# Feed-forward output projection by seven half-size products, with the sums of weights made in DRAM

## The reference, cut to what matters

```
def swiglu(h, w_in, w_out):
    gate, up = jnp.split(h @ w_in, 2, axis=-1)
    return (jax.nn.silu(gate) * up) @ w_out
...
    x = x + 0.5 * swiglu(rmsnorm(x, norm_ffn1[layer]), w_ffn1_in[layer], w_ffn1_out[layer])
```

## Time and profile before

| | us |
|---|---|
| median of 3 runs (1964.11 to 1965.36) | 1964.17 |
| the profiled execution's own time | 1964.59 |
| its span (first to last instruction) | 1962.6 |
| TensorE busy | 1942.2 |
| VectorE busy | 1442.0 |
| ScalarE busy | 891.0 |
| GpSimd busy | 222.1 |

### The profile page before, as it was taken

How to read it: one execution, slowest core, us unless ns; L and a number is a source line. 1 busy time by engine, 2 the same in 40 slices (tenths; PEclk the granted TensorE clock), 3 DMA queues, 4 the chain that set the end, 5 groups by cost and what they waited for, 6 DMA issues and landing times.

```text
span 1962.6 us, 23667 instructions
## 1 busy us (share of the span) xinstructions
PE 1942.2 (99%) x9192; PEld 1616.2 (82%) x9192; DVE 1442.0 (73%) x1815; ACT 891.0 (45%) x1245; POOL 222.1 (11%) x166
## 2 busy tenths in 40 slices
PE   8999999999999999999999999999999999999998
PEld 7888888888888888888888888888897898888886
DVE  7988844886767859898833889883368778988722
ACT  6555632352434435555621555562168445554510
POOL 0000012000000031000021000002146440000121
PEclk9999999999999999999999999999999999999999
DMA  5243122331313320422232242223222014222331
GB/s 173 86 144 114 60 103 91 128 134 43 135 43 134 127 88 12 155 92 86 89 104 86 99 155 92 86 89 103 85 85 86 1 61 155 86 86 101 104 101 60
DMA packets 76188, 189.52 MB, mean 97 GB/s; under 512 B 4144, under 2 KB 12336, under 8 KB 73008
## 3 DMA queue, kind: packets, MB, share of 16 engines
q1 hardware_dynamic: 76080, 188.04, 27.4%
HBM read 185.92 MB, written 2.10 MB: 96 GB/s over the span
## 4 chain that ended last, share of the span: by engine, by line
PE 89%; DVE 6%; issue 2%; ACT 1%; DMA 1%; POOL 1%; SPq 0%; DVEq 0%; ACTq 0%; POOLq 0%
PE bank L2455 12%; PE bank L2457 12%; PE bank L2456 12%; PE bank L2447 12%; PE bank L2449 12%; PE bank L2448 12%; PE bank L2677 3%; PE bank L2675 3%; PE bank L2676 3%; PE bank L2556 2%; DVE part_lo L1567 1%; PE bank L2686 1%; PE bank L2936 1%; PE bank L2875 1%; DVE quad_w L1729 1%
## 5 line engine op out<-in xcount | busy, mean ns | idle before, releaser
L1025 ACT ACTIVATE part_hi<-quad_w 128x1024 fp32r<-128x1024 f32 x280 | 293.3, 1064 | 278.5 <-PE bank L2457 194.5
L1567 DVE TENSOR_TENSOR part_lo<-quad_w,part_hi 128x1024 fp32r<-128x1024 f32 x280 | 330.4, 1221 | 23.6 <-ACT part_hi L1025 23.4
L2447 PE MATMUL bank<-gated_hi,out_hi 128*128 128x512 f32 x704 | 274.8, 390 | 0.0
L2449 PE MATMUL bank<-gated_hi,out_lo 128*128 128x512 f32 x704 | 274.0, 389 | 0.0
L2448 PE MATMUL bank<-gated_lo,out_hi 128*128 128x512 f32 x704 | 273.9, 389 | 0.0
L2455 PE MATMUL bank<-part_hi,s_hi 128*128 128x512 f32 x640 | 252.3, 394 | 1.1 <-DVE part_lo L1567 1.1
L2457 PE MATMUL bank<-part_hi,s_lo 128*128 128x512 f32 x640 | 249.4, 390 | 0.0
L2456 PE MATMUL bank<-part_lo,s_hi 128*128 128x512 f32 x640 | 249.2, 389 | 0.0
L2455 PE MATMUL bank<-part_hi,xn_hi 128*128 128x512 f32 x608 | 237.4, 390 | 2.8 <-DVE part_lo L1567 2.8
L2457 PE MATMUL bank<-part_hi,xn_lo 128*128 128x512 f32 x608 | 236.6, 389 | 0.0
L2456 PE MATMUL bank<-part_lo,xn_hi 128*128 128x512 f32 x608 | 236.6, 389 | 0.0
(11 more groups left out here) (306 smaller groups left out, 3522.9 us busy)
## 6 DMA issues: line engine op xcount, KB each, us to landing
quad_w<-w_ffn_in SPq DMA_DIRECT2D x80, 1024.0 KB, 7.4
out_raw<-w_ffn_out SPq DMA_DIRECT2D x64, 704.0 KB, 4.1
quad_w<-w_ret_in SPq DMA_DIRECT2D x14, 1024.0 KB, 7.4
rest_raw<-w_ffn_in SPq DMA_DIRECT2D x32, 256.0 KB, 5.3
quad_w<-w_ret_in SPq DMA_DIRECT2D x16, 512.0 KB, 5.3
quad_w<-w_ret_out SPq DMA_DIRECT2D x8, 1024.0 KB, 5.3
w_raw<-w_dsa SPq DMA_DIRECT2D x7, 1024.0 KB, 4.8
x_res<-x_in SPq DMA_DIRECT2D x8, 256.0 KB, 6.7
```

The source lines that it names most:

```text
L1025: nc.scalar.activation(in_four(part_hi[part_slot(h)]), source, copy).then_inc(part_hi_made, 1)
L1567: nc.vector.tensor_tensor(in_four(part_lo[part_slot(h)]), source, in_four(part_hi[part_slot(h)]).bitcast(FP32), ALU.subtract)\
L2447: mm(to, w_hi_of[:, at:at + width], hi, start=start, stop=False)
L2449: return mm(to, w_lo_of[:, at:at + width], hi, start=False, stop=stop)
```

## The change

The output product becomes a Strassen scheme too (`OUT_PRODUCTS`, seven products), with halves of the features (11 tiles), of the tokens (256) and of the output columns (4 chunks, `OUT_TILES`). A product is 4 steps (`out_step`), one for each chunk, of 11 tiles x 3 matmuls with 256 tokens moving. Of the seven left factors three are plain quarters of the activations and four are sums; VectorE makes the sums (`sum_left`) and the low parts, ScalarE the high parts. Of the seven right factors three are plain quarters of `w_out`; four are sums of quarters (`T_SUMS`), and no engine computes them. GpSimd issues, for each, one transfer that copies a quarter (or an earlier sum) from DRAM to DRAM and, when it has landed, one that adds a second quarter onto it in DRAM. They start in the input stage. The output stage then loads 28 units of 128 x 1408, from `w_ffn_out` or from `t_sums`, into ten places of memory (`OUT_PLACES`). Three chains of products gather in PSUM, two chunks of 256 tokens to a bank, and 14 or 16 instructions of VectorE (`add_out`) bring them to the residual, some with a minus sign. Squares for the next norm are made by ScalarE (`square`), and summed by VectorE (`add_square`), in three of the four feed-forwards; in the last one GpSimd still squares the first 4 chunks. At the end of the stage VectorE's order is: the last `add_out`, `stream_lo` of chunks 6 and 7, two squares, and then the next stage's first weights (before the attention stage, the unit of 128 x 2048).

```diff
+OUT_PRODUCTS = ("x11w11", "x12w21", "S1T1", "S2T2", "S3T3", "x22T4", "S4w22")
+T_SUMS = ("S1T1", "S2T2", "S3T3", "x22T4")
+T_TERMS = {"S1T1": ("w11", "w12"), "S2T2": ("S1T1", "w22"), "S3T3": ("w12", "w22"), "x22T4": ("S2T2", "w21")}
+OUT_PLACES = "AIBC" + "DEGH" + "ABCD" + "EGHA" + "BCGJ" + "EDFC" + "ABFC"
...
+    t_sums = nc.dram_tensor("t_sums", (SUBLAYERS.count("ffn") * len(T_SUMS) * OUT_TILES, P, OUT_UNIT), FP32).ap()
...
+                if s == 0:
+                    pool.wait_ge(part_lo_made, parts_through(f, 0, PRODUCTS.index("S4w22")))
+                for name in T_SUMS:
+                    first, second = T_TERMS[name]
+                    source = t_units(f, first) if first in T_SUMS else quarter_units(f, first)
+                    nc.gpsimd.dma_start(t_units(f, name), source, max_dma_last_dim=4 * OUT_UNIT)\
+                        .then_inc(t_copied, 16)
+                    pool.wait_ge(t_copied, t_count(f, name))
+                    nc.gpsimd.dma_start(t_units(f, name), quarter_units(f, second), accum_op=ALU.add,
+                                        max_dma_last_dim=4 * OUT_UNIT).then_inc(t_summed, 16)
+                    pool.wait_ge(t_summed, t_count(f, name))
...
+                    if name in T_SUMS and dt == 0:
+                        sp.wait_ge(t_summed, t_count(f, name))
+                    load_out_unit(i)
...
+                    for k in range(HALF_TILES):
+                        if dt == 0 and k in batches:
+                            pe.wait_ge(left_lo_made, left_count(f, p, batches.index(k)))
+                        left_hi_k, left_lo_k = cols(left_hi[p % 2], k, HALF_SEQ), left_low_tile(p, k)
+                        first_in, last_in = opens and k == 0, closes and k == HALF_TILES - 1
+                        w_hi_k, w_lo_k = hi[:, k * P:(k + 1) * P], lo[:, k * P:(k + 1) * P]
+                        mm(to, w_hi_k, left_hi_k, start=first_in, stop=False, skip_group_check=joins)
+                        mm(to, w_hi_k, left_lo_k, start=False, stop=False, skip_group_check=joins)
+                        done = mm(to, w_lo_k, left_hi_k, start=False, stop=last_in, skip_group_check=joins)
+                    done.then_inc(unit_done, 1)
```

More of the change, by code:

```diff
@@ new lines, in add_out @@
+                def add_out(name, p, piece, part, factor):
+                    (a, b), chain = piece, chain_of(p)
+                    n, first = out_bank(s, chain, a)
+                    columns, tokens = {"x11": (0, 0), "x12": (1, 0), "x21": (0, 1), "x22": (1, 1)}[name]
+                    x = x_res[:, :].rearrange("p (k t) -> p k t", k=CHUNKS)
+                    to = x[:, OUT_TILES * columns + a:OUT_TILES * columns + b,
+                           HALF_SEQ * tokens:HALF_SEQ * (tokens + 1)]
+                    made = bank[n][:, :].rearrange("p (d t) -> p d t", d=2)[:, first:first + b - a]
+                    dve.wait_ge(unit_done, u0 + OUT_TILES * p + b)
+                    done = nc.vector.scalar_tensor_tensor(to, made, factor, to, ALU.mult, ALU.add)
+                    if part is None:
+                        done.then_inc(x_updated, b - a)
+                    else:
+                        done.then_inc(x_added, 1)
@@ new lines, in _ @@
+                out_low(14)
+                out_low(15)
+                for piece in pieces(s, "Z")[1:]:
+                    add_out("x22", 2, piece, "P5", 0.5)
+                left_low(4, 0)
+                out_low(16)
+                left_low(4, 1)
+                out_low(17)
+                sum_left("S4")
+                add_out("x12", 3, two[0], "P6", -0.5)
+                out_low(18)
+                out_low(19)
+                add_out("x12", 3, two[1], "P6", -0.5)
+                left_low(5, 0)
@@ new lines, in _ @@
+                for i in range(OUT_STEPS):
+                    if s == len(SUBLAYERS) - 1 and i == OUT_STEPS - 1:
+                        final = ("norm", len(SUBLAYERS))
+                        pe.wait_ge(squares_done, squares_before(final) + square_ops(final))
+                        for b in range(BLOCKS):
+                            done = mm(bank[STAT_BANK][:, b:b + 1], tile(square_sum, b), ones[:, :1],
+                                      start=True, stop=True)
+                        done.then_inc(stat_done, 1)
+                    out_step(i)
+                    if i in (0, 2):
+                        turn(GROUPS - 1, i // 2)
```

602 lines of the change are left out of this document (402 added, 200 removed).

## The result

The kernel after takes 1997.08 us (median of 4 runs, 1994.67 to 2000.22) where the kernel before takes 1964.37 in runs beside it: 1.0166 times as long, 95% interval 1.0149 to 1.0184. I had forecast 1930 and a range up to 1990. It is slower, by 1.7%. The profiled execution has a span of 1992.8 us against 1962.6: 30.2 more.

What follows compares the result with a forecast made beforehand. TensorE was taken as the bound, with work in flight for 1942.2 of 1962.6 us. 1964.59 - 36.3 (matmuls) + 1.7 (seam) = 1930.0 us, with the transfers in DRAM counted as hidden; range 1923 to 1990.

Steps and rivals of the forecast that it cites:

- Matmuls, 9.1 us a stage: Output stages: 924 matmuls at 0.1197 us replace 528 at 0.2267, a gain of 9.1 us a stage, 36.3 in all.
- VectorE, 13.4 to 14.2 of 15.8 us: Output stage: VectorE's work per middle product, 13.4 to 14.2 us, fits in TensorE's 15.8 us, so no stall.
- two thin covers: Output stage: VectorE readies the second product's activations 1 to 2 us early and the fifth's bank about 1 us early.
- the rival in which VectorE binds: Output stage: three-dimensional operands or thin covers cost VectorE 5 to 10%, 3 to 8 us a stage, 1940 to 1965; chance 0.17.
- The step that doesn't halve: Rival: output matmuls take 0.1295 us or more, the change gains nothing or loses, 1964 to 1975; chance 0.04.
- The sums come late: Rival: transfers need over 28 us each, TensorE stands at the fourth to sixth products, 2007 to 2200; chance 0.07.
- The seams, +1.7: Into attention the second weight unit is ready 8.0 us after the last matmul, TensorE there at 6.3: +1.7 us, once.
- The very end: End of kernel: last add half as wide, -0.3 us, four squares where one stood; nothing counted.
- I take no loss: Input stages: the DRAM transfers, 162 us per eight, delay no burst of quads; cover 7 us, loss none.
- VectorE wants the first two at 118.17 and the third at 124.03: Input stage: when VectorE needs the quads of a burst that SP issues from 98.37.
- With half the rate left to them: Input stage: beside transfers the first two quads land at 111, the third at 116, hidden with 7 us cover.
- the quads come late: Rival, input stages: row-by-row sharing leaves quads 27%, 107 GB/s; +100 to +160 us, or with pauses 1980 to 2010; chance 0.17.

Runs made afterwards that it cites:

- e10: e2 with each pair of transfers issued when the third quad of a burst has landed, not the fourth: 1934.09 us, 0.9843 of before.
- e1: The kernel after without its 32 transfers in DRAM, plain quarters loaded in place of the sums: 1934.45 us, 0.9843 of before.
- e2: The kernel after with each pair of transfers (copy, add) issued only once the fourth quad of a burst has landed: 1940.70 us, 0.9874 of before.
- e8: e2 with each pair of transfers issued as a burst of quads begins, not as it has landed: 1974.32 us, 1.0054 of before.
- e17: The kernel after with each copy issued when a burst of quads has landed, each add as the next burst begins: 2071.65 us, 1.0542 of before.

## Why the forecast was wrong

**Matmuls, 9.1 us a stage: right.** 0.120 us from start to start, 9.05 to 9.31 a stage, 36.7 in all against 36.3.

**VectorE, 13.4 to 14.2 of 15.8 us: right.** Busy 93.5 of 112.7 us (I had said 95 to 100), `out_lo` 1.62 us, 1.75 for 1536 columns (1.76 forecast), 3.08 for 2816. TensorE waits for nothing in the output stages, so the two thin covers held, and the rival in which VectorE binds is out.

**The step that doesn't halve: out.** **The sums come late: out.** A copy landed in 11 to 15 us and an add in 17 to 23, against estimates of 16.7 and 23.9; the eight of the first stage began at 61.12, ten us sooner than I had, and the last, issued at 179.98, landed 17.1 us later, at 197, so 136 us in place of 162, and 53 before the output stage.

**The seams, +1.7: about right.** In the kernel whose quads are in time (e10) the stretch through attention is 1.3 us longer than before, 1.1 of it TensorE's wait for `w_lo`. (It is 2.8 and 3.0 longer in e1 and e2, with the same wait; what the rest is stays open.) The first two input stretches are 0.9 longer each, which I had not counted; the third is even.

**The very end, "I count nothing": mis-sized, +3.9 us.** The last add ends 0.3 us sooner, but `mean_sq` then follows 4.5 us after it, before 1.8, and the last stream starts 1.4 us later behind it. 1930.0 + 3.9 + 1.8, less 0.4 (the seam) and 0.3 (the output stages, 36.6 in e10), is 1935.0; the profiled execution of e10 took 1934.8, so the account closes.

**"I take no loss" for the quads: the step that failed,** with the two sentences that it stands on. Both are wrong.

The first is "VectorE wants the first two at 118.17 and the third at 124.03". Those are the second and the third sum of a group. Its first sum adds the second quad to the first, and rows 9 leave it out. In the trace of before it starts 12.7 us after the burst's first issue at 98.37, not 19.8:

```profile
111.11 2.35 DVE L1729 TENSOR_TENSOR quad_w<-quad_w,quad_w 128x1024 f32<-128x1024 f32 x2
```

The second is "With half the rate left to them the first two (2.1 MB) land at 98.4 + 10.5 + 2.3 = 111, the third at 116: hidden, cover 7 us". With the right row, 111 has no cover at all. And half the rate is not left: while both queues have rows the quads get 111 GB/s beside a copy and 64 beside an add. The same sum of VectorE where the burst meets a copy (e8, burst from 106.01) and an add (e17, burst from 152.41), with its wait:

```profile
120.77 2.36 DVE L1948 TENSOR_TENSOR quad_w<-quad_w,quad_w 128x1024 f32<-128x1024 f32 x2 [1.93 <-DMA quad_w<-w_ffn_in]
```

```profile
172.44 2.36 DVE L1949 TENSOR_TENSOR quad_w<-quad_w,quad_w 128x1024 f32<-128x1024 f32 x2 [7.21 <-DMA quad_w<-w_ffn_in]
```

Means over the sixteen bursts that have a group ahead of them in their stage, us after the burst's first issue (the first sum is wanted at 12.7 in fifteen of them):

```
                        second quad landed   first sum started   VectorE idle before it
before                          8.0                12.4                 0
e10, a quad ahead               8.9                12.5                 0
e2, behind a burst             11.2                12.9                 0.1
e8, copies meet bursts         14.3                14.4                 1.8
e17, adds meet bursts          18.9                19.0                 6.1
```

The time lost follows this column: 2.5 us a burst in e8 and 8.6 in e17, 40 and 137 in all. A late first sum puts off what VectorE does next and so the issue of the next burst, and no burst makes it up. An add holds the engines longer than a copy, 512 rows x 0.44 us / 16 = 14 us against 7, which is an estimate from the windows above; the difference of 7 is about that between the two losses, 6.1. The free running kernel meets copies, adds and the pauses between, and has 63. Adds had most of its time, 65.5 of the 103.4 us from 61.12 to 164.49, and there the later quads of a burst are late as well (30.9 us to landing, ScalarE waiting 67.2 us for them).

Of the 60 us between the spans of after and e10, 44 are TensorE's waits in the three rows of the section on the result (46.8, and 3.1 in e10), and 12 are longer matmuls: the six groups of `part` matmuls are busy 1475.4 us in all in the kernel after and 1463.3 in e10, at a granted clock of 0.990 and 0.997. So here idle stretches cost TensorE their length and something of its clock.

**The rival "the quads come late"** had the sign, the place, the releaser and the mechanism: row by row, 27% of the bytes, 107 GB/s, where 111 were measured beside a copy. It didn't know that the row of an add holds an engine twice as long, and its point of decision, 120 GB/s, had the same wrong row in it: by 111.11 it is 2.1 MB in 10.4 us, 200 GB/s (an estimate). "With the pauses between the eight transfers" it even had the time, 1980 to 2010. That is partly luck, since it halved a price that e8 and e17 put at 40 to 137 us. I gave it 0.17 because the median quad landed in 6.7 us, "so there is room between the bursts". There is: all of the loss went away once the transfers were put into it. But nothing in the kernel put them there.

## What to carry to other kernels

A background transfer that is hidden by its sum of time can still cost on every burst of loads that it meets: compare it with the slices in which the loads come, not with the mean share, and tie its start by a semaphore to the landing of a burst, which here turned 1.7% slower into 1.6% faster with one wait. Where one is needed, keep the adding transfers furthest from the loads, and look at the outermost dimension of the view before anything else. And before a load is called covered, find the first instruction that reads it: one row of VectorE, left out of the rows, was the difference between 7 us of cover and none. Where loads are issued by the work on the last ones, the lateness of each burst adds up.

## What the runs showed of the hardware

- A transfer from DRAM to DRAM of 2.88 MB with 128 rows outermost landed in 11 to 12 us on free engines and in 16 to 18 beside a burst of quads; an adding one in 17 on free engines and in 22 to 23 beside a burst. On free engines it had 73% of the 16 engines' time in an 11.5 us window with a copy (after, 1107 to 1118.5), 87% of a 17 us one with an add (after, 180 to 197).
- While two queues had rows, they went row for row: 278 of quads (2048 bytes) for 276 of a copy and 378 for 374 of an add (5632 bytes), 119 for 117 with 8192, 553 for 556 with 4224. The quads moved 409 GB/s alone, 111 beside the copy, 64 beside the add. With adds in rows of 352 bytes it was 1,029 for 1,028 in one stretch and 182 for 1,482 in another.
- With the outermost dimension 2 or 4, transfers that were not contiguous on both sides took 60 us for 1.44 MB and 64 us for 2.88; with 88, 23.5 us for 2.88.
- The limit on a row's length counts bytes. It cut the rows of the adding transfers to it (2816, 352) and not those of the copies (5632 at a limit of 2816, 4224 at one of 352).
- With the adds in rows of 352 bytes and the copies in rows of 4224, q0 took 30.5% of the engines' time for bytes that took 18.3% in rows of 5632.
